# Layer 1's input norm weight multiplied into the weight pieces instead of the transposed tokens

## The reference, cut to what matters

```python
def rms_norm(x, w):
    xf = x * lax.rsqrt(jnp.mean(x * x, axis=-1, keepdims=True) + RMS_EPS)
    return xf * w

# layer 1
h = rms_norm(x, norm_mix_w[1])
q, k, v, g = split_cols(h @ w_in, (1024, 1024, 2048, 2048))
q, k = rotary(split_heads(q, 4)), rotary(split_heads(k, 4))
o = multiscale_retention(q, k, split_heads(v, 4))
x = x + merge_heads(rms_norm(o, norm_w) * silu(split_heads(g, 4))) @ w_out
x = x + hierarchical_moe(rms_norm(x, norm_ffn_w[1]), ...)
```

## Time and profile before

| what | value |
|---|---|
| median of 3 runs | 1178.77 us (1173.87 to 1180.03) |
| the profiled execution, its own time | 1179.09 us |
| its span, first to last instruction | 1177.3 us |
| mean granted TensorE clock | 0.981 of full speed |
| busy: PE / DVE / ACT / POOL | 1130.4 / 696.8 / 609.4 / 395.4 us |
| layer 1's projection and retention on TensorE | 590 to about 855 us |

### The profile page before, as it was taken

How to read it: one execution, slowest core, us unless ns; L and a number is a source line. 1 busy time by engine, 2 the same in 40 slices (tenths; PEclk the granted TensorE clock), 3 DMA queues, 4 the chain that set the end, 5 groups by cost and what they waited for, 6 DMA issues and landing times.

```text
span 1177.3 us, 19837 instructions
## 1 busy us (share of the span) xinstructions
PE 1130.4 (96%) x7119; PEld 923.7 (78%) x7119; DVE 696.8 (59%) x1014; ACT 609.4 (52%) x905; POOL 395.4 (34%) x344
## 2 busy tenths in 40 slices
PE   8999999999998899998999999999999997999996
PEld 5788887777787788886788888888888886788873
DVE  5436434377737999996646341543432137999984
ACT  5556334342425599995633333233342234899982
POOL 5344121110123243332155325443235431344432
PEclk9999999999999899999999999999999997999998
DMA  9333211111225789996443213332222263999955
GB/s 263 78 88 67 61 45 49 37 55 55 72 79 199 272 331 376 383 362 233 168 134 92 87 54 108 90 101 69 81 73 90 91 204 137 358 380 377 382 213 223
DMA packets 81667, 194.76 MB, mean 165 GB/s; under 512 B 20348, under 2 KB 21432, under 8 KB 80824
## 3 DMA queue, kind: packets, MB, share of 16 engines
q1 hardware_dynamic: 59368, 159.34, 40.1%
q10 hardware_dynamic: 12432, 17.60, 4.4%
q0 software_dynamic: 9792, 16.80, 3.8%
HBM read 189.50 MB, written 23.07 MB: 181 GB/s over the span
## 4 chain that ended last, share of the span: by engine, by line
PE 86%; DVE 6%; ACT 3%; DMA 2%; issue 2%; ACTq 1%; POOL 0%; DVEq 0%; POOLq 0%
PE ps L679 24%; PE ps L681 23%; PE ps L680 23%; PE ps L2586 2%; PE ps L2378 2%; PE ps L2125 1%; PE ps L2215 1%; PE ps L2261 1%; ACTq L1436 1%; DMA arena<-hs,slot_rows 1%; PE ps L2514 1%; DMA arena<-y 1%; PE ps L2651 1%; PE ps L2158 1%; ACT wh L1012 0%
## 5 line engine op out<-in xcount | busy, mean ns | idle before, releaser
L846 POOL TENSOR_TENSOR wl<-raw,wh 128x1024 fp32r<-128x1024 f32 x94 | 229.7, 2450 | 378.3 <-ACT wh L1012 378.0
L679 PE MATMUL ps<-wh,hT_hi 128*128 128x512 f32 x864 | 348.0, 403 | 2.4 <-DVE hT_lo L2002 2.4
L681 PE MATMUL ps<-wh,hT_lo 128*128 128x512 f32 x864 | 338.7, 392 | 0.0
L680 PE MATMUL ps<-wl,hT_hi 128*128 128x512 f32 x864 | 338.4, 392 | 0.0
L1012 ACT ACTIVATE wh<-raw 128x1024 fp32r<-128x1024 f32 x116 | 122.4, 1067 | 211.7 <-PE ps L681 190.4
L679 PEld LDWEIGHTS ps<-wh,hT_hi 128*128 128x128 f32 x864 | 163.5, 189 | 37.4 <-DVE hT_lo L2002 2.9
L681 PEld LDWEIGHTS ps<-wh,hT_lo 128*128 128x128 f32 x864 | 162.9, 189 | 34.6
L680 PEld LDWEIGHTS ps<-wl,hT_hi 128*128 128x128 f32 x864 | 163.4, 189 | 31.1 <-issue 0.2
L679 PE MATMUL ps<-hT_hi,wh 128*128 128x512 f32 (+1 forms) x296 | 116.4, 393 | 2.8 <-issue 1.1
L1977 DVE TENSOR_TENSOR wl<-arena,wh 128x1024 fp32r<-128x1024 f32 x96 | 113.6, 1222 | 5.7 <-ACT wh L1303 5.4
L1977 DVE TENSOR_TENSOR wl<-raw,wh 128x1024 fp32r<-128x1024 f32 x92 | 109.3, 1222 | 8.3 <-ACT wh L1303 6.1
(11 more groups left out here) (339 smaller groups left out, 1596.0 us busy)
## 6 DMA issues: line engine op xcount, KB each, us to landing
raw<-in_moe_w_gate_up_dram SPq DMA_DIRECT2D x64, 512.0 KB, 10.1
arena<-in_moe_w_gate_up_dram SPq DMA_DIRECT2D x64, 512.0 KB, 9.6
raw<-in_odd_w_in_dram SPq DMA_DIRECT2D x48, 512.0 KB, 3.7
raw<-in_even_w_in_dram SPq DMA_DIRECT2D x32, 512.0 KB, 4.8
arena<-in_moe_w_down_dram SPq DMA_DIRECT2D x32, 512.0 KB, 10.4
raw<-in_moe_w_down_dram SPq DMA_DIRECT2D x32, 512.0 KB, 13.6
raw<-in_odd_w_out_dram SPq DMA_DIRECT2D x16, 512.0 KB, 3.4
arena<-y ACTq DMA_DIRECT2D x6, 1024.0 KB, 9.8
```

The lines of the kernel that those rows point to most:

```text
L679: nc.tensor.matmul(dst, lh, rh, start=first, stop=False)
L680: nc.tensor.matmul(dst, lh, rl, start=False, stop=False)
L681: return nc.tensor.matmul(dst, ll, rh, start=False, stop=last)
L846: pool.tensor_tensor(columns_of(i, wl[:, i % NSPL, :, :]), raw_columns(i), columns_of(i, wh[:, i % NSPL, :, :]).bitcast(F32), ALU.subtract ...
```

## The change

The norm weight is no longer multiplied into `HTH` and `HTL`. The 48 pieces of blocks 10 to 21 take it instead.

- **Tokens.** ACT and DVE write each transposed PSUM tile in one instruction of 128 x 512 (8 on each engine in place of 32).
- **Block 10's four pieces.** Their high halves are two ACT instructions of 128 x 512 with `nw1`'s column as scale, and their low halves two DVE instructions of 128 x 512. The fourth piece moves: ACT makes its high half after the loads of `YP` are issued, and DVE its low half after the first tile is combined.
- **The 44 pieces of blocks 11 to 21.** A new function `fold_norm` on ACT multiplies the piece in its raw slot, in place, in two instructions of 128 x 512, each waited for. It runs one piece ahead of `hi`: four times in `norm(2)` (block 11's pieces), and after each `hi` of the steps of blocks 11 to 20. High and low halves are then made as before.
- TensorE's, POOL's and SP's instructions keep their order.

```diff
+        def norm_folded(i):
+            return first_piece(10) <= i < first_piece(22)
+        def folded_columns(i):
+            k = 2 * ((i - first_piece(10)) % 4)
+            return [nw1[:, k + k2:k + k2 + 1] for k2 in range(2)]
...
             def hi(i):
...
+                if norm_folded(i) and lo_by_dve(i):
+                    act.wait_ge(s_("wb_loaded"), 32)
+                    w = folded_columns(i)
+                    A(act.activation(wh[:, i % NSPL, 0, :], raw_at(i)[:, 0, :], ACT.Copy, scale=w[0]))
+                    act.activation(wh[:, i % NSPL, 1, :], raw_at(i)[:, 1, :], ACT.Copy, scale=w[1]).then_inc(hi_done, 1)
+                    return
+            def fold_norm(i):
+                if not norm_folded(i):
+                    return
+                act.wait_ge(raw_loaded[RAW_SLOTS[i]], 16 * raw_load(i))
+                for x, w in zip((raw_at(i)[:, 0, :], raw_at(i)[:, 1, :]), folded_columns(i)):
+                    A(act.activation(x, x, ACT.Copy, scale=w))
...
-                    if n == 2:
-                        for j in range(4):
-                            k = 4 * g + j
-                            A(act.activation(HTH[:, k, cols(T)], tile(name)[:, cols(j)], ACT.Copy, scale=nw1[:, k:k + 1]),
...
             def norm(n):
                 if n == 2:
                     transposed(n, 0)
                     for T in range(NT):
                         if T + 1 < NT:
                             transposed(n, T + 1)
                         square(n, T)
+                        if T > 0:
+                            fold_norm(first_piece(10) + T + 3)
                     roots()
+                    fold_norm(first_piece(10) + 7)
...
-                for i in range(4):
+                for i in range(3):
                     hi(m + 6 * NE + i)
...
                     act.dma_start(YP[:, T, :, :], src[T]).then_inc(s_(f"yp_loaded{T}"), 16)
+                hi(m + 6 * NE + 3)
...
                     for i in splits_at(step):
                         hi(i)
+                    if k == "piece":
+                        fold_norm(first_piece(step[1]) + step[2] + 4)
...
             def norm(n):          # DVE
-                    for i in range(4):
+                    for i in range(3):
                         lo(first_piece(10) + i)
                     combine(0, 0, 0)
                     combine(0, 0, 1)
+                    lo(first_piece(10) + 3)
                     combine(0, 1, 0)
...
             def lo(i):            # DVE
+                if norm_folded(i):
...
+                    D(stt(low[:, 0, :], r[:, 0, :], w[0], hi[:, 0, :], ALU.mult, ALU.subtract))
+                    stt(low[:, 1, :], r[:, 1, :], w[1], hi[:, 1, :], ALU.mult, ALU.subtract).then_inc(lo_dve, 1)
```

More of the change, by code:

```diff
@@ L1031, in transposed @@
                     tile_is_ready(act, name)
-                    if n == 2:
-                        for j in range(4):
-                            k = 4 * g + j
-                            A(act.activation(HTH[:, k, cols(T)], tile(name)[:, cols(j)], ACT.Copy, scale=nw1[:, k:k + 1]),
-                              s_("hT_hi_made") if j == 3 else None)
-                        continue
                     A(act.activation(HTH[:, 4 * g:4 * g + 4, cols(T)], v3(tile(name), 4), ACT.Copy), s_("hT_hi_made"))
@@ L1041, in norm @@
                 if n == 2:
-                    act.wait_ge(s_("wb_loaded"), 32)
                     transposed(n, 0)
@@ L1490, in norm @@
                     combine(0, 0, 1)
+                    lo(first_piece(10) + 3)
                     combine(0, 1, 0)
                     combine(0, 1, 1)
-                    dve.wait_ge(s_("wb_loaded"), 32)
                     for T in range(NT):
@@ L1582, in lo_tiles @@
                     hi, lo = (x[:, 4 * g:4 * g + 4, cols(T)] for x in ((HTH2, HTL2) if name[0:3] == ("yT", 1, 0) else (HTH, HTL)))
[L1583 to L1591, removed]
+                    if name[0:2] == ("yT", 0):
                         D.read(stt(lo, v3(tile(nm), 4), head_w[:, g:g + 1], hi.bitcast(F32), ALU.mult, ALU.subtract), nm)
@@ L1774, in lo @@
                 wait_spl_free(dve, i)
+                if norm_folded(i):
+                    w = folded_columns(i)
+                    hi, low, r = (x.bitcast(F32) if n == 0 else x for n, x in enumerate((wh[:, i % NSPL, :, :], wl[:, i % NSPL, :, :], raw_at(i))))
+                    D(stt(low[:, 0, :], r[:, 0, :], w[0], hi[:, 0, :], ALU.mult, ALU.subtract))
+                    stt(low[:, 1, :], r[:, 1, :], w[1], hi[:, 1, :], ALU.mult, ALU.subtract).then_inc(lo_dve, 1)
+                    return
                 tt(wl[:, i % NSPL, :, :], raw_at(i), wh[:, i % NSPL, :, :].bitcast(F32), ALU.subtract).then_inc(lo_dve, 1)
```

## The result

The changed kernel takes 1180.7 us (median of 20 runs, 1177.75 to 1185.07) against 1178.78 (20 runs, 1173.87 to 1182.01): 1.9 us more. The ratio is 1.0023, 95% interval 1.0013 to 1.0033. A second series of 12 runs gave 1.0029 (1.0014 to 1.0044). Both intervals exclude 1, so the change costs about 0.25%, which lies within the 0.5% that the prediction called no change. The profiled execution took 1183.03 us (span 1181.2).

What follows compares the result with a forecast made beforehand. TensorE, busy 1130.4 of 1177.3 us, was taken as the bound, so ACT or DVE work counts only where TensorE waits. Terms + 1.93 + 0.6 + 1.7 = + 4.2 on 1179.09 gave 1183.3, median 1183.0 us, range 1177 to 1186.

Steps and rivals of the forecast that it cites:

- The fold (f = 1.50): ACT's two 128 x 512 instructions multiplying a raw piece by the norm weight: 1.50 us per fold, bounds 1.33 and 1.65.
- The chain and the wait before block 11: ACT's chain behind the last tile: three added folds start block 10's reading 1.93 us late; TensorE idles 2.46 instead of 0.95.
- removed tokens -1.96: ACT's token writes in fewer, longer instructions: 1.96 us less per tile, shortening the chain only on tile 3.
- Tile 1, +0.42: DVE's low half of the fourth piece between tiles 0 and 1: tile 1 starts 0.42 us late, bounds 0.2 to 0.5.
- The loads, "take nothing": Loads of the expert results, issued by ACT after three high halves: no delay taken, upper bound 0.35 us.
- Blocks 14 and 20, 2 x 0.3: Ends of blocks 13 and 19: a fold delays ACT's reading, overdrawing the slack by 0.3 us each, 0.6 us together.
- The clock, +1.7 in two of three: After the longer idle time before block 11, TensorE's clock falls in two of three executions, costing 1.7 us each.
- The sum: Whole kernel against the profiled execution of 1179.09: + 1.93 + 0.6 + 1.7 = + 4.2 us, 1183.3; median of runs 1183.0.
- the likeliest case: The forecast itself, clock fall included: whole kernel 1183.0 us, own range 1181 to 1185.5, chance 0.5.
- rival A: All as forecast, but the clock holds at 593, before block 11: 1178.8 + 2.5 = 1181.3 us, chance 0.3.
- (B): Folds delay the start of each of blocks 11 to 21, up to 1.5 us each: 1197 us, chance 0.07.
- (C): Faster: the last tile's shorter tokens win over the folds if f is below 0.86 us: 1176.1 us, chance 0.13.

## Why the prediction held

**The fold (f = 1.50).** Right. The instruction takes 0.723 us (predicted 0.72) and the step is 1.51. All 88, with ns min/median/max:

```profile
L1035 ACT ACTIVATE raw<-raw,vec x88: 705/723/728, 576.3 to 847.3; 128x512 f32<-128x512 f32 x88
```

The estimate by the Trainium skill (ScalarE: Activation LUTs, section What ACT_TABLE_LOAD costs) was 0.71 for the instruction, 2% under the measured value.

**The chain and the wait before block 11.** Right. ACT's reading comes 14.41 us after the last tile's first token write (predicted 14.3), the idle time is 2.56 (predicted 2.46). The steps in it, removed tokens -1.96 and POOL's gap covered, are shown apart: the first by the short tokens (+1.92), the second by the timeline without folds, where the gap of 1.03 is back.

**Tile 1, +0.42.** Wrong in sign: tile 1's wait went from 1.90 and 1.84 to 1.50 and 1.63, 0.3 us less on the mean. The step said "DVE ends tile 0 at 558.28 and stands 1.14 us until 559.43", and put 1.56 us of work into 1.14 of idle time. That work is where it was said, but what bounded tile 1 before was the landing of its load, and this came earlier. DVE after, in answer to the earlier trace rows:

```profile
559.69 2.60 DVE L1504 SCALAR_TENSOR_TENSOR x<-arena,small,x 128x1024 f32<-128x1024 f32 x2 [3.10 <-DMA arena<-y]
562.33 0.75 DVE L1792 SCALAR_TENSOR_TENSOR wl<-raw,vec,wh 128x512 fp32r<-128x512 f32 x1
563.12 0.75 DVE L1793 SCALAR_TENSOR_TENSOR wl<-raw,vec,wh 128x512 fp32r<-128x512 f32 x1
563.79 2.60 DVE L1504 SCALAR_TENSOR_TENSOR x<-arena,small,x 128x1024 f32<-128x1024 f32 x2
```

Tile 0's two halves run without the 1.43 us between them, and tile 1 without a wait for a DMA. It starts 563.79 - 555.15 = 8.64 us after the first load's issue, where it was 559.43 - 550.05 = 9.38. The term was taken from one landing time as if it were fixed. Why the loads land earlier is open, but it goes with the move of the fourth piece: with the piece ahead of the loads again, tile 1 was back at 9.57.

**The loads, "take nothing".** Nearly right: issued 5.42 us after the last expert matmul's start in place of 5.14, 0.28 later, within the bound of 0.35.

**Blocks 14 and 20, 2 x 0.3.** Right, in the places, which were the only ones, and nearly in the size. ACT's timeline at the end of block 13 answers to the earlier trace rows:

```profile
668.51 1.06 ACT L1027 ACTIVATE wh<-raw 128x1024 fp32r<-128x1024 f32 x1
669.48 1.47 ACT L1035 ACTIVATE raw<-raw,vec 128x512 f32<-128x512 f32 x2
670.98 2.86 ACT L1271 ACTIVATE arena_rounded<-ps,small 128x512 fp32r<-128x512 f32 x4
```

The reading starts 2.47 us behind the start of `hi`, before it was 0.96: the fold's 1.5, as estimated. From the start of `hi` to block 14's first matmul are 4.16 us (672.67 - 668.51), before they were 3.83 (668.06 - 664.23): 0.33 more, as predicted. The list of waits says 0.16 because it counts idle time from the modelled end of the matmul before. TensorE's pace is the distance between starts, and that is 0.23 us in these blocks; here it is 0.55:

```profile
672.12 0.39 PE L690 MATMUL ps<-wh,hT_lo 128*128 128x512 f32 x1
672.67 0.47 PE L688 MATMUL ps<-wh,hT_hi 128*128 128x512 f32 x1 [0.16 <-DVE arena_rounded L1854]
672.97 0.39 PE L689 MATMUL ps<-wl,hT_hi 128*128 128x512 f32 x1
```

The next step is 0.30 and so 0.08 too long as well, which the prediction didn't count. One place costs 0.4, both cost 0.8. The transposes inside block 21, before and after, confirm it:

```profile
857.83 1.91 PE L2261 MATMUL ps<-ident,arena 128*128 128x128 f32 x16
```

```profile
862.99 1.91 PE L2281 MATMUL ps<-ident,arena 128*128 128x128 f32 x16
```

From block 11's first matmul these are 265.84 us before and 266.67 after (265.82 and 266.65 in the second profile of each): 0.83 us for the 40 folds.

**The clock, +1.7 in two of three.** Not settled, and probably too high. Of five profiles with a wait of 2.55 or 2.56 us, two show the lower level behind it (the fourth piece ahead, no block folds) and three don't. Two falls of 1.7 us in five are 0.7 on the mean, and 1.1 were implied. Over all runs, the time lost to the clock is 21.7 +- 0.6 us in the changed kernel (32 runs) and 21.2 +- 0.4 before (75 runs): 0.5 +- 0.7 more. The price per fall was a little high for this place: without folds in the blocks, where the clock falls behind the wait, block 14's first matmul comes 77.39 us after block 11's, and 76.07 before, so the fall cost 1.3. A counterweight was missed: both profiles of before show the lower level behind tile 1's wait (1.90, 1.84), and neither of the changed kernel does (1.50, 1.63).

**The sum.** The profiled execution took 3.9 us more and the sum was 4.2, but that agreement is luck: most of the 3.9 lay ahead of the boundary. The fair comparison is over runs. Less the time lost to the clock, the changed kernel's mean is 2.0 +- 0.45 us above before (1158.92 against 1156.95). The traces say 1.61 for block 11, 0.83 for the blocks and -0.3 for tile 1, in sum 2.1, which accounts for it; the prediction's terms were 1.93 + 0.6 = 2.5. With the clock it was 2.5 us, where the likeliest case said 4.2 and rival A 2.5. So of the two the rival came nearer on the mean, and both profiles of the changed kernel are its case: the clock holds behind the wait. That rival A's number is met exactly is luck too, since its +0.42 at tile 1 had the wrong sign and some of the clock's mean stands in for it.

**The rivals.** (B), every block delayed, is refuted: only blocks 14 and 20 start late, by 0.4 us each. With the folds doubled, 1.5 us more per piece, still only four places pay. (C), faster, hung on f below 0.86; it is 1.51. But the thought behind it, that the shorter tokens can win, came true once the folds are out of the chain: the wait falls to 0.55, under the 0.95 of before.

## What to carry over

In this kernel, work that was added to an engine at half load cost nothing except at the few places where that engine's queue is the chain which ends a wait. There it costs its length less whatever slack is left, and all of its length once there is none. So find these places in the timeline, put nothing new in them, and fill the idle time of the same engine a few microseconds ahead, where one step of slack is enough. Read the cost of a small wait from the distance between starts, not from the listed idle time alone. And before a difference of 4 us between two profiles is explained, look at whether a second profile of the same kernel moves by as much.

## What the runs showed of the hardware

- **The clock after an idle stretch.** The same idle time of 2.56 us, at the same place of the program, was followed by a granted clock of 0.76 or 0.77 over 7 us (half speed for part of it) in two profiles and of 1.00 in three. The window of the changed kernel, and that of the kernel without folds in the blocks, each from the first matmul behind the wait:

```profile
596.00:603.00 7.00, 6.68 (x30) 5.58 (x31) 3.79 (x6) 4.78 (x7) 6.36 (x3) 1.00 0.76 222
```

```profile
588.00:595.00 7.00, 6.64 (x23) 5.42 (x24) 3.83 (x6) 2.65 (x4) 6.37 (x3) 0.77 0.74 222
```

  Waits of 1.84 to 2.10 us at tile 1 were followed by it in all three profiles that had one, waits of 1.35 to 1.63 there in none, and 4.48 us before block 11 in the one that had it. Yet in all 13 profiles TensorE stood 1.81 to 1.90 us behind the experts, and the clock fell there in one alone, the one with the fourth piece ahead. So the length of an idle time does not decide it. What a fall costs shows in that profile: the same 44 matmuls took 13.80 us in place of 12.11, 1.7 more.
- **DMA issues on ACT's queue.** The three loads of 1 MB take 1.65 to 1.81 us to issue in both profiles of before and with the fourth piece ahead, and 2.0 to 2.9 in the others (2.49 in the changed kernel's first profile). In those kernels tile 0's second half and tile 1 landed earlier. That the later loads start later and leave the earlier ones more of the bandwidth would fit; why the issue takes longer stays open, and no run tells it.
- **The part ahead of the boundary** moved by 5.4 us between two profiles of one kernel, and by 7.6 us between four kernels on one chip that are alike up to there. That is more than any effect of this change.
